# Taking the up projection of a gated feed-forward block out of PSUM before the gate product is formed

## The reference, cut to what matters

```
def swiglu(h, w_gate, w_up, w_down):
    return (jax.nn.silu(h @ w_gate) * (h @ w_up)) @ w_down

for layer in range(DEPTH):                      # DEPTH = 2
    f = swiglu(rms_norm(h, g[0]), ffn_w_gate[layer, 0], ffn_w_up[layer, 0], ffn_w_down[layer, 0])
    h = h + 0.5 * rms_norm(f, g[1])
    ...                                         # the mixer of the layer
    f = swiglu(rms_norm(h, g[4]), ffn_w_gate[layer, 1], ffn_w_up[layer, 1], ffn_w_down[layer, 1])
    h = h + 0.5 * rms_norm(f, g[5])
```

## Time and profile before

| | |
|---|---|
| median of 3 runs | 3460.56 us (3459.33 to 3468.28) |
| the profiled execution's own time | 3468.28 us |
| its span | 3466.5 us |
| busy: PE, DVE, ACT, POOL | 3200.9, 1555.1, 1156.0, 1166.6 us |
| the four feed-forward parts in the span | about 20 to 400, 580 to 930, 950 to 1325, 1700 to 2090 us |

### The profile page before, as it was taken

One profiled execution on the slowest core, in us unless ns is written; L12 is line 12 of the kernel. 1 busy time (PEld: TensorE's weight loads), 2 busy tenths in 40 slices (PEclk: granted clock), 3 DMA queues, 4 the chain that ended last, 5 costly groups with the idle time before them and its releaser, 6 DMA issues.

```text
span 3466.5 us, 54028 instructions
## 1 busy us (share of the span) xinstructions
PE 3200.9 (92%) x20656; PEld 2413.3 (70%) x20656; DVE 1555.1 (45%) x3123; ACT 1156.0 (33%) x1979; POOL 1166.6 (34%) x982
## 2 busy tenths in 40 slices
PE   7999999999999999999899998888989988789888
PEld 5888677787687786777687787666656666556555
DVE  3232664222632236444522146665564356664644
ACT  3222333222422223111322135443435344444443
POOL 3444353444344443222244443230331113222212
PEclk9999999999999999999999999888989999889999
DMA  3222222323223331111133332000001111001011
GB/s 134 97 97 97 85 80 81 140 97 139 97 101 136 128 112 70 55 62 56 60 109 127 136 107 86 32 14 25 33 25 62 37 58 52 32 19 44 26 50 55
DMA packets 74357, 264.67 MB, mean 76 GB/s; under 512 B 7856, under 2 KB 9136, under 8 KB 73904
## 3 DMA queue, kind: packets, MB, share of 16 engines
q1 hardware_dynamic: 67104, 242.25, 19.7%
q10 hardware_dynamic: 7056, 19.69, 1.5%
HBM read 252.47 MB, written 7.34 MB: 75 GB/s over the span
## 4 chain that ended last, share of the span: by engine, by line
PE 75%; DVE 12%; issue 7%; ACT 3%; POOL 2%; DMA 0%; ACTq 0%; DVEq 0%; POOLq 0%
PE ps L1401 57%; PE ps L1897 3%; PE ps L1920 2%; PE ps L1870 2%; POOL wl L932 1%; DVE tb L2587 1%; PE ps L1763 1%; PE ps L1479 1%; PE ps L1702 1%; PE ps L1950 1%; PE ps L1460 1%; ACT tb L1297 1%; DVE work L2390 1%; PE ps L1783 1%; DVE tb L2212 1%
## 5 line engine op out<-in xcount | busy, mean ns | idle before, releaser
L932 POOL TENSOR_TENSOR wl<-raw,wh 128x1024 fp32r<-128x1024 f32 x320 | 771.1, 2410 | 1199.2 <-ACT wh L1036 718.4
L1401 PE MATMUL ps<-xh,wh 128*128 128x512 f32 x2400 | 908.5, 403 | 92.1 <-POOL wl L920 31.0
L1401 PE MATMUL ps<-xl,wh 128*128 128x512 f32 x2400 | 859.2, 382 | 0.0
L1401 PE MATMUL ps<-xh,wl 128*128 128x512 f32 x2400 | 858.2, 382 | 0.0
L1401 PEld LDWEIGHTS ps<-xh,wh 128*128 128x128 f32 x2400 | 440.6, 195 | 254.5 <-issue 151.0
L1036 ACT ACTIVATE wh<-raw 128x1024 fp32r<-128x1024 f32 x224 | 237.6, 1061 | 976.2 <-PE ps L1401 906.4
L920 POOL TENSOR_TENSOR wl<-raw,wh 128x1024 fp32r<-128x1024 f32 x90 | 220.6, 2451 | 909.9 <-ACT wh L1014 902.9
L1401 PEld LDWEIGHTS ps<-xl,wh 128*128 128x128 f32 x2400 | 439.6, 194 | 92.8 <-issue 13.4
L1401 PEld LDWEIGHTS ps<-xh,wl 128*128 128x128 f32 x2400 | 437.1, 193 | 86.6
L1401 PE MATMUL ps<-ah,wh 128*128 128x512 f32 x1104 | 437.1, 403 | 12.6 <-issue 11.2
L1401 PE MATMUL ps<-al,wh 128*128 128x512 f32 x1104 | 418.1, 386 | 0.0
(11 more groups left out here) (351 smaller groups left out, 3616.0 us busy)
## 6 DMA issues: line engine op xcount, KB each, us to landing
raw<-wts_dram SPq DMA_DIRECT2D x458, 512.0 KB, 3.4
spilled_dram<-hc ACTq DMA_DIRECT2D x1, 3072.0 KB, 8.8
hc<-spilled_dram ACTq DMA_DIRECT2D x1, 3072.0 KB, 10.0
tb<-tab_dram ACTq DMA_DIRECT2D x5, 512.0 KB, 3.6
hc<-x_dram ACTq DMA_DIRECT2D x8, 256.0 KB, 9.1
spilled_dram<-hc ACTq DMA_DIRECT2D x1, 2048.0 KB, 7.2
hc<-spilled_dram ACTq DMA_DIRECT2D x1, 2048.0 KB, 8.3
out_dram<-hc SPq DMA_DIRECT2D x8, 256.0 KB, 2.1
```

Source lines behind the costliest of these rows:

```text
L932: pool.tensor_tensor(wl[:, n % SPLIT, :], raw[:, LOADED[n] % RAW, :], wh[:, n % SPLIT, :].bitcast(F32), ALU.subtract).then_inc(lo_done, 1)
L1401: ins = pe.matmul(out_, w[:, s, k * P:(k + 1) * P], x_(k, at), start=first, stop=last)
```

## The change

The up tile is scaled by `r` out of PSUM into `tt[:, j, :]` in SBUF, and `taken` is counted by that instruction. The two products and the subtraction then work on `tt` in place of the PSUM bank. The wait of DVE on its own scaling is on `taken` instead of `dve_own` (which is now counted twice and not three times for a chunk), and the wait on `a_ready` with the separate increment of `taken` behind it is gone.

```
-                    s0, o0, a0 = c.take("sil", part), c.take("own", 3 * part), c.take("a", part)
+                    s0, o0, a0 = c.take("sil", part), c.take("own", 2 * part), c.take("a", part)
                     with dve.Fori(0, part // 2) as it:
                         for j in range(2):
...
                             dve.wait_ge(tile_done, it * 4 + (n0 + 2 * j + 1))
                             dve.tensor_tensor(sil[:, j, :], ps[:, (n0 + 2 * j) % 4, :], r, ALU.mult).then_inc(taken, 1)
-                            up = ps[:, (n0 + 2 * j + 1) % 4, :]
                             dve.wait_ge(tile_done, it * 4 + (n0 + 2 * j + 2))
-                            dve.tensor_tensor(up, up, r, ALU.mult).then_inc(dve_own, 1)
+                            dve.tensor_tensor(tt[:, j, :], ps[:, (n0 + 2 * j + 1) % 4, :], r, ALU.mult).then_inc(taken, 1)
                             dve.wait_ge(sil_ready, it * 2 + (s0 + j + 1))
-                            dve.wait_ge(dve_own, it * 6 + (o0 + 3 * j + 1))
-                            dve.tensor_tensor(hi, up, sil[:, j, :], ALU.mult).then_inc(dve_own, 1)
-                            dve.tensor_tensor(up, up, sil[:, j, :], ALU.mult).then_inc(dve_own, 1)
-                            dve.wait_ge(dve_own, it * 6 + (o0 + 3 * j + 3))
-                            dve.tensor_tensor(lo, up, hi.bitcast(F32), ALU.subtract).then_inc(a_ready, 1)
-                            dve.wait_ge(a_ready, it * 2 + (a0 + j + 1))
-                            dve.sem_inc(taken, 1)
+                            dve.wait_ge(taken, it * 4 + (n0 + 2 * j + 6))
+                            dve.tensor_tensor(hi, tt[:, j, :], sil[:, j, :], ALU.mult).then_inc(dve_own, 1)
+                            dve.tensor_tensor(tt[:, j, :], tt[:, j, :], sil[:, j, :], ALU.mult).then_inc(dve_own, 1)
+                            dve.wait_ge(dve_own, it * 4 + (o0 + 2 * j + 2))
+                            dve.tensor_tensor(lo, tt[:, j, :], hi.bitcast(F32), ALU.subtract).then_inc(a_ready, 1)
```

## The result

| | before | changed |
|---|---|---|
| median of the first 4 runs each | 3464.42 us (3459.33 to 3473.29) | 3490.11 us (3487.13 to 3493.35) |
| ratio | | 1.0070 (1.0053 to 1.0087) |
| mean of all runs, those of the experiments included | 3468.8 us (64) | 3489.2 us (43) |

The account below looks back on a forecast made before the run. PE was taken as the bound. Eight stops of 0.78 us and four of 2.13 sum to 14.8 us, which on a base of 3460.6 gives 3475.4, stated as 3476; the range was 3463 to 3485.

Parts of the forecast that it names:

- The bound and the place: Feed-forward parts: PE never waits there; the change makes it stop only at the last chunk of groups' first down tiles.
- The exclusion, its order and its length: Up tiles: DVE steps with two SBUF inputs alternate with POOL; second product 2.8 to 2.9 us, low part at 5.14.
- Rival C: Up tiles: queued DVE steps hold off POOL, whose late remainder stops PE four times, 4 us, 3465; chance 0.17.
- The twelve stops: Group ends: PE waits for the late low part, 8 x 0.78 and 4 x 2.13 us, 14.8 in all.
- No gain from the early release: Up tile's PSUM bank: free some 2.3 us earlier, but PE does not wait for it; gain 0.
- rival D: Feed-forward matmuls: faster through less PSUM use by DVE or the bank freed earlier; price 0, 3460.6 us, chance 0.05.
- The step on the clock: Behind the four last-group stops: a slower clock could cost 0 to 6.8 us; taken as 0, 6.8 kept for the range.
- Rival B: Same stops plus a slower clock behind those of 2.1 us: up to 21.6 us, 3482; chance 0.16.
- The base: Whole kernel: the time before the change, taken as 3460.6 us, the median of three runs.

Follow-up runs that it names:

- e6_split: The changed kernel with POOL's remainder made by two instructions of 512 columns instead of one of 1024: 3478.4 us, 1.0031 of the kernel before.
- the two runs with bank 7: Against the kernel before, the scaled up tile goes to PSUM bank 7 and its bank is freed early; run twice: 3470.8 and 3467.6 us (1.0011, 0.9997).
- SBUF free late: The changed kernel's SBUF buffer for the scaled up tile, but the PSUM bank set free late as in the kernel before: 3484.2 us, 1.0049.
- SBUF in the last group: The kernel before with the SBUF buffer only in the last group of each feed-forward part, bank set free late: 3480.4 us, 1.0034.
- the delay: The kernel before with three more DVE products, one SBUF input each, between high part and full value: 3479.9 us, 1.0037.
- the long stop: The kernel before with five more DVE products ahead of the full value, in the last group only: 3482.7 us, 1.0042.
- SBUF in one kind of group: Two kernels: the one before with the SBUF buffer only in the last group (3480.4 us) or only in the first two groups (3474.3 us) of each part.

## Why the prediction was right or wrong

**The bound and the place: right.** PE was the bound, the only new waits are the twelve at the last chunk of a group's first down tile.

**The exclusion, its order and its length: right.** Scaling, first product, POOL, second product, subtraction in this order; 2.65 for POOL (2.65 said), 2.89 for the second product (2.8 to 2.9 said), the low part at 5.14 (5.14 said). Rival C (DVE's queued step goes before the waiting POOL) is dead: the second product was issued right behind the first, but 0.30 us after POOL had asked (123.66 and 123.36), and came after POOL. `e6_split` shows that the turn is a whole instruction.

**The twelve stops: right.** 0.77 and 2.1 against 0.78 and 2.13; 14.6 us against 14.8. No gain from the early release: right, by the two runs with bank 7. So rival D is gone too.

**The step on the clock: wrong.** I set it at 0 because a gap of 1.82 us had been followed by the full clock, and read that one case as a rule. It was one draw. The same wait, at the same place of unchanged code, stands in twelve of the thirteen traces (1.81 to 1.83 us), and in five of them 3.4 us at 1.2 GHz begin 1.0 to 2.0 us behind it (a wait of 0.32 us lies between), for example in a second trace of the changed kernel (PE in order of time, then the stretch of 3.4 us):

```profile
1373.10 1.10 PE L1625 MATMUL ps<-work,cn 128*128 128x512 f32 x2 [1.82 <-DVE work L2267]
...
1375.10:1378.50 3.40, 3.40 (x10) 2.63 (x9) 2.36 (x4) 0.00 (x0) 0.00 (x0) 0.50 0.00 0
```

At the stops it is the same. Over the five traces with waits of 1.83 us (the changed kernel three times, SBUF free late, SBUF in the last group) 9 of 20 such waits were followed by 3.4 us at 1.2 GHz; with waits of 1.72 and 1.59 us it was 0 of 8, with 3.19 us 4 of 4. One fall costs about 1.6 us, so the term should have been 4 x 9/20 x 1.6 = 3 us. One row told me that the fall need not come, not that it won't; the right value was a share. Rival B, with a chance of 0.16, had this mechanism, at up to 6.8 us.

**The base: wrong.** "In runs like the median one" took 3460.56, the median of three runs. The mean of 64 runs is 3468.8, 8 us higher, with single runs from 3459 to 3479. The profiled execution (3468.28), which I called the slowest of three, was the typical one. This step alone put the time, 3490, outside the range: on a base of 3468.8 the same range would have ended at 3493. Of the 14.7 us between the sum (3475.4) and the measured 3490.1, 8.2 are the base and 3 the clock, the stops take 0.2 away, and 3.7 are left.

**What stays open.** Over all runs the change costs 20.4 us with an error of 0.9, and 14.6 + 3 explain 17.6 of it. The 3 is shown at its place in the traces, not in the totals. At equal clock the 43 runs are 18.7 ± 0.5 over the kernel before, still 4 more than the stops, and the kernel with SBUF and the late release is 18.2; the delay, the long stop and SBUF in one kind of group lie within 1.5 us of their stops. What the 4 us are, no trace shows: up to 2090 us PE is idle for 79.1 to 79.6 us before and with bank 7 (three traces) and for 89.8 to 90.6 in the three of the changed kernel, which is its twelve waits and no more. The stage behind the feed-forward parts, from 2080 us on, has between 206 and 234 us at 1.2 GHz in the thirteen traces, with the same code; by the line over the 60 runs (2.2 us for 0.001 of the clock, which is 6.9 us at 1.2 GHz) about a third of such time is lost, so some 9 us of difference between executions. Why the long stops show 20 us in their trace and cost 14, and whether stops move the later falls of the clock in a lawful way, I can't say from these runs.

## What to carry to other kernels

Before a value moves from PSUM to SBUF, count the SBUF inputs of each VectorE instruction that will read it: with two, it takes turns with GpSimd's SBUF work, and its length becomes what is left of GpSimd's instruction and 0.54 us (0.69 became 2.89 here), so a free PSUM bank is the better scratch (bank 7 here, no cost). What a delay off the bound costs is decided at the few places where the bound wants the result soon: 76 of 88 chunks show no wait of PE, 12 paid all that a trace shows. And a forecast of half a percent needs a base from more than three runs, times compared at equal clock where runs have it on record, and a share, not a yes or no, for whether the clock falls behind a stop near 2 us.

## What the runs showed of the hardware that was not expected

Waits of PE of the same length (1.83 us) in the same place of the same kernel are followed by 1.2 GHz in some executions and by 2.4 GHz in others (part (0,1): twice 1.2, once 2.4 in three traces of the changed kernel). More than half of the variance between runs of one kernel goes with the mean granted clock, which moves by a few thousandths (correlation -0.76 over 60 runs). And a POOL instruction cut in two lets VectorE in between: the product between the halves was 1.11 us shorter (2.89 to 1.78), while the step behind it grew by 0.88 (0.69 to 1.57).
